# A one-core encoder layer: stick-breaking scans moved into PSUM, depthwise convolution shared by three engines, layer norm moved between attention steps

## What is computed

```
u = a_val * jax.nn.sigmoid(a_gate)
a_out = silu(layernorm(causal_dwconv(concat(conv_hist, u), conv_w, conv_b), ln_g, ln_b))   # 512 channels, 31 taps
...
vis = s[None, :] < t[:, None]                      # strictly causal
log_keep = where(vis, log_sigmoid(-z), 0.0)        # z = q.k / 8, 8 heads of 64
later = cumsum(log_keep, reverse=True) - log_keep
w = where(vis, exp(log_sigmoid(z) + later), 0.0)
b_out = head_rmsnorm(w @ v, g_sb)
...
x = x + concat(a_out, b_out) @ w_out
x = x + hier_moe(rmsnorm(x))                       # top 2 of 8 experts in the best of 4 groups
```

## Time and profile before

| | |
|---|---|
| median of 3 runs | 611.93 us (610.77 to 612.71) |
| the profiled execution | 612.33 us, its span 610.6 us |
| busy share of the span | PE 87%, DVE 50%, ACT 23%, POOL 17% |
| chain that ended last | PE 46%, DMA 19%, DVE 15%, "issue" 13% |
| DMA share, last 16 of 40 slices | 90% or more in 15 of them |

### The profile page before, as it was taken

The page is one execution under the profiler, slowest core; times in us unless marked ns, Lnnn a source line. Parts: engine busy times, 40 slices in busy tenths (PEclk is TensorE's granted clock), DMA queues, the critical chain, the costliest instruction groups (busy, mean ns, idle before and its releaser), DMA issues.

```text
span 610.6 us, 7803 instructions
## 1 busy us (share of the span) xinstructions
PE 529.4 (87%) x3155; PEld 332.7 (54%) x3156; DVE 306.6 (50%) x496; ACT 143.3 (23%) x228; POOL 100.8 (17%) x110
## 2 busy tenths in 40 slices
PE   6999999998983895995999979999999987678994
PEld 5779999997552664743465564344443432233331
DVE  2853999996997699123545873111111101111147
ACT  4421212213462481203320210010100100000013
POOL 2100000000454364010110220111111111111003
PEclk9999999998598596998799969999999989999997
DMA  8806564205208000084454569999999999999995
GB/s 291 213 1 203 178 194 151 70 1 169 80 2 308 10 2 0 4 343 181 146 208 172 187 218 408 425 420 424 422 423 422 422 422 423 420 424 419 415 371 167
DMA packets 44763, 148.93 MB, mean 244 GB/s; under 512 B 7124, under 2 KB 23532, under 8 KB 36279
## 3 DMA queue, kind: packets, MB, share of 16 engines
q1 hardware_dynamic: 40263, 139.63, 59.1%
q0 software_dynamic: 4464, 8.80, 3.8%
HBM read 136.29 MB, written 19.59 MB: 255 GB/s over the span
## 4 chain that ended last, share of the span: by engine, by line
PE 46%; DMA 19%; DVE 15%; issue 13%; SPq 4%; ACT 2%; POOL 1%; DVEq 0%; POOLq 0%; ACTq 0%
DMA big<-in_w_expert_out 12%; PE ps L1120 10%; PE ps L1300 9%; PE ps L1325 5%; DVE big L1855 4%; PE ps L914 4%; DVE big L1782 4%; PE ps L879 3%; DMA cw<-h_dram,low 2%; SPq L619 2%; DMA out<-low 2%; PE ps L1034 2%; PE ps L1281 2%; DMA y_dram<-cw,low 1%; PE ps L867 1%
## 5 line engine op out<-in xcount | busy, mean ns | idle before, releaser
L1782 DVE SCALAR_TENSOR_TENSOR big<-low,cwt,big 128x590 f32<-128x590 f32 x120 | 96.3, 852 | 0.3
L2115 DVE TENSOR_TENSOR low<-low,ps 128x256 f32<-128x256 f32 x16 | 6.7, 422 | 172.6 <-ACT low L1631 172.6
L1300 PE MATMUL ps<-big,low 128*64 128x512 f32 x320 | 85.0, 593 | 5.0 <-issue 4.0
L914 PE MATMUL ps<-cw_r 128*128 128x280 f32 x256 | 72.3, 292 | 0.0
L914 PE MATMUL ps<-low_r,cw_r 128*128 128x280 f32 x256 | 72.2, 292 | 0.0
L914 PE MATMUL ps<-cw_r,big_r 128*128 128x280 f32 x256 | 72.1, 291 | 0.0
L1120 PE MATMUL ps<-cw,low 128*128 128x512 f32 x128 | 61.3, 635 | 5.2 <-ACT low L1581 4.4
L1300 PEld LDWEIGHTS ps<-big,low 128*64 128x64 f32 x320 | 29.8, 137 | 47.3 <-issue 47.2
L1325 PE MATMUL ps<-big,low 128*64 128x512 f32 x160 | 43.8, 597 | 11.9 <-DMA big<-in_w_expert_out 5.3
L1855 DVE TENSOR_TENSOR_SCAN big<-big 128x512 f32<-128x512 f32 (+4 forms) x42 | 42.6, 1054 | 10.7 <-ACT big L1508 10.7
L914 PEld LDWEIGHTS ps<-cw_r 128*128 128x128 f32 x256 | 47.2, 188 | 0.4 <-issue 0.4
(11 more groups left out here) (265 smaller groups left out, 771.7 us busy)
## 6 DMA issues: line engine op xcount, KB each, us to landing
big<-in_w_expert_in SPq DMA_DIRECT2D x16, 2048.0 KB, 18.8
big<-in_w_expert_out SPq DMA_DIRECT2D x20, 1024.0 KB, 25.5
big<-in_w_in SPq DMA_DIRECT2D x20, 512.0 KB, 5.2
low<-in_w_expert_out SPq DMA_DIRECT2D x8, 1024.0 KB, 30.9
low<-in_w_expert_in SPq DMA_DIRECT2D x4, 2048.0 KB, 22.7
cw<-in_w_expert_in SPq DMA_DIRECT2D x4, 2048.0 KB, 26.3
low<-in_w_expert_in SPq DMA_DIRECT2D x4, 1536.0 KB, 22.8
big<-in_w_expert_in SPq DMA_DIRECT2D x6, 1024.0 KB, 32.1
```

The costliest lines, as they stand in the source:

```text
L914: return pe.matmul(ps[:, proj_bank(j) + half, 0:PROJ], w[:, k, :], h[:, k, cols], start=first, stop=last, skip_group_check=True)
L1300: mm = pe.matmul(ps[TILE * half:TILE * half + TILE, gu_bank(g), :], xt[:, k, TILE * half:TILE * half + TILE], wi_at(2 * g + half, k), star ...
L1782: ins = dve.scalar_tensor_tensor(conv[:, i, :], u[:, i, j:j + CW], cwt[:, i, j:j + 1], conv[:, i, :], ALU.mult, ALU.add)
```

## The change

- The sigmoid of -z stays where the scores are: ACT writes it over the scores in PSUM, the scan runs in place there, and DVE (no longer POOL) multiplies the product in PSUM by the sigmoid of z into `wts`. From 384 keys on, each head has its own ACT instruction (four a step for two). `keep` and `left` are gone; the carry of the few-row steps is two columns of `stat`. A pair of banks is free only when that product is written (`w_ready`).
- Of the 30 taps left for attention DVE does 4. For the other 26, ACT writes weight times shifted input into one of four SBUF buffers (`product`) and POOL adds it to `conv` (`tap`). The convolution's bias goes into tap 0, and the last taps write `yc` themselves.
- Layer norm becomes three positions of `order`: `ln_mean` behind the 384-key steps, `ln_var` behind the second 512-key step, `ln_spread` between the third and fourth. The variance is formed with 20 matmuls with one column each, POOL takes its root, five matmuls spread it over partitions, DVE scales all four blocks in two instructions. ACT's Silu comes at position NQ, beside the last step.
- PE transposes weights two positions after the scores (it was three) and sums values after three; the heads' outputs are normalised straight from PSUM; POOL adds eps to the heads' means.
- The K copy at position 15 waits for the stores of the first K output alone. SP issues the first two experts' weights before the router's and behind the Silu, and no longer between the stores of h2.

```diff
-TAPS_STEP = (1,) * 30
-TURN_LAG, SUM_LAG, OUT_LAG = 3, 4, 5
-MEANS_LAG, ROOT_LAG, NORM_LAG, IN_LAG = 6, 7, 8, 9
+STEP_TAPS = 4
+POOL_TAPS = (8, 10, 7)
+PRODUCTS = (1, 1, 1, 1, 2, 1, 1, 2, 1, 1, 2, 2, 1, 2, 1, 2, 1, 1, 1, 1)
+TURN_LAG, SUM_LAG = 2, 3
+SQUARE_LAG, MEANS_LAG, NORM_LAG, OUT_LAG = 4, 4, 6, 7
...
-        order = groups[0] + [dict(ko=0)] + groups[1] + [dict(ko=1)] + groups[2] + [dict(ko=2)] + groups[3] + groups[4]
+        order = groups[0] + [dict(ko=0)] + groups[1] + [dict(ko=1)] + groups[2] + [dict(ko=2)] + groups[3]
+        order += [ln_mean] + groups[4][0:2] + [ln_var, groups[4][2], ln_spread, groups[4][3]]
...
+            sp.wait_ge(mixa_ready, NI)
+            load_wi(0)
             load_router()
+            load_wi(1)
             load_wi(2)
...
+            def tap(n):
+                i, j = taps[n]
...
+                t = product_of(n)
+                pool.wait_ge(product_ready, n - taps_by_dve + 1)
+                if j < TAPS - 1:
+                    pool.tensor_tensor(conv[:, i, :], t, conv[:, i, :], ALU.add).then_inc(pool_tap_done, 1)
...
+            for g in range(3):
+                for n in range(marks[g], marks[g + 1]):
+                    tap(n)
+                head_root(g)
+            for n in range(marks[3], marks[4]):
+                tap(n)
+            root(ln_stat)
...
                 gone = order[q - 2]
                 if "n" in gone:
-                    pe.wait_ge(beta_ready, gone["s"] + 1)
+                    pe.wait_ge(w_ready, gone["s"] + 1)
...
+            def mean(st):
+                bank_free(st["q"])
+                pe.wait_ge(yc_ready, NI)
+                pe.wait_ge(pool_tap_done, NI * TAPS - taps_by_dve)
...
+                for a in range(2):
+                    z = ps[:, bank + a, 0:n]
+                    act.activation(t[:, a], z, ACT.Sigmoid).then_inc(beta_ready, 1)
+                    act.activation(z, z, ACT.Sigmoid, scale=-1.0).then_inc(keep_ready, 1)
...
-                act.wait_ge(ko_stored, 16 * 4)
+                act.wait_ge(ko_stored[0], 16 * 2)
...
+            def product(n):
...
+                if n - taps_by_dve >= 4:
+                    act.wait_ge(pool_tap_done, n - taps_by_dve - 3)
+                act.activation(product_of(n), u[:, i, j:j + CW], ACT.Copy, scale=cwt[:, i, j:j + 1]).then_inc(product_ready, 1)
...
-                    dve.tensor_tensor_scan(t[:, a, lo:lo + n][:, ::-1], k, k, start, ALU.mult, ALU.min).then_inc(left_ready, 1)
+                    dve.tensor_tensor_scan(k, k, nones[:, 0:1].broadcast_to([P, n]), carry[:, a:a + 1] if cached else 1.0,
+                                           ALU.mult, ALU.max).then_inc(left_ready, 1)
...
+                dve.tensor_tensor(w[:, :, 0:n - 1], ps[:, bank:bank + 2, 1:n], w[:, :, 0:n - 1], ALU.mult).then_inc(w_ready, 1)
```

More of the change, by code:

```diff
@@ L446, in build, with tap_order @@
         OUT_BANK = (2, 4, 6, 2, 6)
+        def tap_order():
+            left, last, units = [TAPS] * NI, None, NI
+            turns = [n for i in range(NI) for n in [i + 1] * TAPS_EARLY[i]]
+            for n in range(NI * TAPS):
+                units = turns[n] if n < len(turns) else NI
+                others = [i for i in range(units) if left[i] and i != last]
+                last = max(others, key=lambda i: left[i]) if others else last
+                yield last, TAPS - left[last]
+                left[last] -= 1
+        taps = list(tap_order())
+        taps_by_dve = sum(TAPS_EARLY) + STEP_TAPS
+        product_of = lambda n: part(592 * (n % 4), CW)
+        tap_before = {n: taps.index((i, j - 1)) for n, (i, j) in enumerate(taps) if j}
         proj_bank = lambda j: 2 * (j % 4)
+        LN_ROOT = NC + 3 + 1
         block = ctx.enter_context(nc.Block())
@@ L1571, in _ @@
                     copy_ko(order[q])
+                for _ in range(PRODUCTS[q] if q < len(PRODUCTS) else 0):
+                    product(products.pop(0))
+                if q < NQ and q and order[q - 1] is ln_mean:
+                    for i in range(NI):
+                        deviation_square(i)
+                if q == NQ:
+                    act.wait_ge(ko_stored[1], 16 * 2)
+                    act.wait_ge(ko_stored[2], 16 * 2)
+                    act.wait_ge(norm_ready, 2)
+                    for i in range(NI):
+                        act.activation(mixt[:, i, :], yc[:, i, :], ACT.Silu, bias=vt[:, 16 + i:17 + i],
+                                       scale=vt[:, 12 + i:13 + i]).then_inc(mixa_ready, 1)
@@ L1572, in _ @@
                 if step_at(q - TURN_LAG):
                     copy_weights(step_at(q - TURN_LAG))
-            outputs(NC - 1)
-            act.preload_act_table_set("natural_log_exp_and_others")
-            for i in range(NI):
-                deviation_square(i)
-            ln_roots()
-            for i in range(NI):
-                act.wait_ge(norm_ready, i + 1)
-                act.activation(mixt[:, i, :], yc[:, i, :], ACT.Silu, bias=vt[:, 16 + i:17 + i],
-                               scale=vt[:, 12 + i:13 + i]).then_inc(mixa_ready, 1)
+            assert not products
@@ L1585, in copy_h2t @@
+            output_squares(NC - 1)
             def copy_h2t(c):
@@ L1840, in normed @@
[L1840 to L1855 removed]
+                tap()
```

341 lines of the change are left out of this document (167 added, 174 removed).

## The result

The changed kernel takes 591.25 us (median of 4 runs, 590.17 to 592.3); the kernel before, run beside it, 611.35. The ratio is 0.9668 (95% interval 0.9642 to 0.9694). That is 20 us less where I had forecast 30 less (582, range 568 to 598). The profiled execution took 592.3, its span 590.6.

What follows compares the result with a forecast made beforehand. Saturated weight transfers bound the experts, so only the stages ahead could shrink, bound by DVE, short chains and PE. A -11.7, B +12, C -31 give -30.7 from 612.3: 582 us predicted, range 568 to 598.

Steps and rivals of the forecast that it cites:

- Stage A: Attention from 143 to 214.7 us, to the last 384-key step: 60 us instead of 71.7, bounds 53 and 72.
- The hole: In attention, 193 to 200 us, only a transfer runs while ACT's third K copy waits for stores; 7 us to go.
- Scan in PSUM: DVE's scan of 512 elements in PSUM: 1.21 us, at most 2.42; the skill page's fixed costs would add 4 us overall.
- Stage B: The 512-key steps, 214.7 to 238.7 us, interleaved with the layer norm's chain: 36 us instead of 24, bounds 28 and 46.
- T: End of the last 384-key product, from which the times of the 512-key steps, mean and variance are counted.
- upper bound of 46: Upper bound for the 512-key steps: PE's 17 us in that chain at a clock of 0.63.
- Stage C: Heads' norms, layer norm and projection, 238.7 to 343.7 us: 74 instead of 105, bounds 71.5 and 85.
- Transfers: Expert weights' prefetch still fits ahead of the experts; the saturated stage stays 212 us long, starting near 332.
- Held banks: Rival in attention: score banks held until DVE's product serialise the steps, 72 and 46 us for the two parts; 603, chance 0.17.
- POOL's pace: Rival in attention: POOL's sums set the pace, deciding from 2.1 us a sum; 630 at 4 us; chance 0.03.
- Nothing for the end: Rival: the experts' weights' stream doesn't start earlier, so the time stays 612; chance 0.03.
- Full overlap: Rival: attention's two parts and the projection stretch take 53, 30 and 71.5 us, 46 less, giving 566; chance 0.13.

Runs made afterwards that it cites:

- sumsq: Changed kernel with POOL adding the four blocks of squares, so PE's variance sums one block with 10 instructions instead of 40: 589.14 us, ratio 0.9656.
- order_alone: Changed kernel, long sums kept, reordered: one 512-key step before the mean, variance behind the third, spread behind the fourth; projection not waiting for the norm: 590.25 us.
- mixed_copy: Changed kernel with shorter mean and variance sums, one 512-key step before the mean, and ScalarE's turned-weights copy before the four Silus: 577.01 us, ratio 0.9444.
- sbuf_scan: Changed kernel with the products' scans back in SBUF and score banks free once ScalarE has read them: 603.17 us, ratio 0.9877.
- ln_last: Changed kernel with the layer norm's three positions behind all four 512-key steps: 587.13 us, ratio 0.9603.

## Why the prediction was right in direction and 9 us too low

**Stage A: forecast 60, measured 63.0.** The hole goes, as forecast, but was priced too low: there is no pause of 7 us near 195, and the two runs on that wait price it at 9 us alone and 12 within the change, where I had put 7. The engines' sums held too: DVE 48.9 (52), POOL 39.0 (39), PE 47.9 (53.2). Mis-sized was ScalarE's product: 0.789 for 0.69, over 26 products 2.6 us, which puts ScalarE, the busiest engine of A, at 51.7. The other term is the loss of three engines that pass steps around: I took 7 over the busiest engine, from no row, and A took 11.3 over it. No run separates the two. DVE's sum also left out the scans of the last 384-key step (1.79), since the earlier trace rows cuts A ahead of them; by one and the same event A fell by 12.6 and B grew by 22.1.

**Scan in PSUM: held.** 1.218, with SBUF at 1.212: 6 ns apart. The 4 us by the fixed costs of the Trainium skill (VectorE: DVE Perf Modes, section on the TRN2 errata) don't appear; of the two readings the rows' was the right one. What I had not priced is what the kernel would have lost otherwise: with scans and products in SBUF, beside POOL's taps, 9 us in A.

**Stage B: forecast 36, measured 42.1; this step failed.** Counted from T = 205.99, the chain was right up to the mean (T+0.8 for T+1.4). The terms were the mean, 3.9, and the variance, 40 times 0.12, both taken at the full clock: they took 6.67 and 8.64, mostly at the lower level (granted clock 0.60 and 0.50). Step one ended at T+15.4 (13.9), step two at T+20.4 (19.6), the variance at T+26.8 (21.2), step four at T+42.1 (36). So by step two most of the mean's 2.8 us were made up by terms that came out shorter than forecast; from the variance on 6 us are missing: 3.9 are its own length, the rest what stands ahead of it. The lower clock stood in my upper bound of 46, not in the sum, although showed 0.71 in A. The runs with shorter sums show that these two terms are what B waits for: 42.1 falls to 34.4 with the shorter variance and a mean that took 4.12, and to 33.7 with the shorter mean as well. The run with the norm behind shows that I hadn't asked whether the four steps need wait at all (15.2).

**Stage C: forecast 74, measured 74.5, in part by luck.** PE runs without a gap, row block 4 takes the 7.04 that was expected, and L1170 is at the full clock. But one piece of the projection is missing from my sum. Row block 0 comes in three pieces:

```profile
248.28 3.65 PE L1170 MATMUL ps<-cw,low 128*128 128x512 f32 x8
...
252.64 3.60 PE L1170 MATMUL ps<-cw,low 128*128 128x512 f32 x8
...
257.81 7.08 PE L1170 MATMUL ps<-cw,low 128*128 128x512 f32 x16
```

I had the first (3.45) and the last (6.9), not the second: L1170 has 128 instructions and my sum 120. With it the work at full clock is some 75, and the 2.5 us that I added for a recovering clock weren't needed in this order (1.00); the two errors nearly cancel. In sumsq and order_alone, where B was shorter, part of the first projections did run at the lower clock: C grew by 3.3 and 6.9, the latter with the wait for a copy.

**Transfers: held.** The saturated stage is 212.6 long, and from row block 4's end to the first expert matmul it is 22.1 (21.7 before). It starts 20 us earlier than before, near 342 where I had 332; the difference is what A and B missed.

**The rivals.** Held banks (603): scans in SBUF free the banks early and B gains 1.7, so there this is no large cost; in A it isn't settled. POOL's pace: 1.335 a sum, far from the 2.1 from which it decides. Nothing for the end: of the 21.0 us saved ahead of the router 20.0 arrived at the end (612.3 to 592.3). Full overlap (566): B was never near 30 in the order of the change; mixed_copy reaches 27.1 and 577.

**Open.** What sets the moment at which the clock falls is not settled: the same mean took 4.12, 5.81 and 6.67 in three executions, and one kernel's executions differed by 11 us with their mean clock. No run held PE busy on purpose there.

## What to carry to other kernels

Interleaving a serial chain with pipelined steps pays where each link's inputs are ready when its turn comes in the fixed order: a link that waits holds the steps of every engine behind it, so put a step ahead of it, and shorten the link with an engine that is idle there. Here the two were worth 11 us together, 6 and 1.5 alone. A saving in one stage must be read again at the next one's start: order_alone won 8 us in B and paid 7 in C, through one copy queued behind unrelated work and a clock that had fallen. Price PE's small instructions in a stage with waits at both clock levels, and take the likelier one into the sum.

## What the runs showed of the chip

- VectorE's scan costs the same from PSUM and SBUF (1218 and 1212 ns for 512 elements), and only the SBUF form is stretched by POOL: scans of 128 to 512 had means of 840 to 1873 ns in stage A of sbuf_scan where the changed kernel has 414 to 1277 in its own, and POOL's sums rose with them from 1335 to 1670.
- A matmul of one column feels the clock, as one of 288 columns does: the variance's 40 instructions took 5.05 us with the clock mostly full (ln_last) and 8.64 at the lower level, the mean's 16 took 4.10 (ln_last) and 6.67 at a granted clock of 0.60.
